# Low parts of the GLU blocks on VectorE, and the first terms of the gate weight sums on SyncE's DMA queue

## What is computed

```
proj = x @ w_in + b_in                  # columns: GLU input (2 x 512) | q | k | v | gate logits (2 x 1024)
u = a * sigmoid(g)                      # a, g: the two halves of the GLU input
u = causal depthwise conv of width 31 over u, + b_dw        # 512 channels
y_conv = silu(layer_norm(u)) @ w_conv_out
y_attn = chunked attention (q, k, v) @ w_attn_out
mixed = (sigmoid(gate_1) * y_conv + sigmoid(gate_2) * y_attn) @ w_o + b_o
x = layer_norm(ALPHA * x + mixed); then a grouped mixture of 16 experts, top 2, and layer_norm again
```

## Time and profile before

| | |
|---|---|
| median of three runs | 1167.88 us (1163.9 to 1169.31) |
| the profiled execution | 1162.02 us, its span 1160.2 us |
| TensorE matmuls | 1082.0 us, 93% |
| VectorE | 827.7 us, 71% |
| ScalarE | 556.4 us, 48% |
| GpSimd | 390.0 us, 34% |
| mean granted clock of TensorE | 0.971 |
| DMA | 222.68 MB, mean 192 GB/s |

### The profile page before, as it was taken

One profiled execution on the slowest core, in us unless ns is written; L12 is line 12 of the kernel. 1 busy time (PEld: TensorE's weight loads), 2 busy tenths in 40 slices (PEclk: granted clock), 3 DMA queues, 4 the chain that ended last, 5 costly groups with the idle time before them and its releaser, 6 DMA issues.

```text
span 1160.2 us, 17229 instructions
## 1 busy us (share of the span) xinstructions
PE 1082.0 (93%) x5487; PEld 897.8 (77%) x5488; DVE 827.7 (71%) x1186; ACT 556.4 (48%) x854; POOL 390.0 (34%) x326
## 2 busy tenths in 40 slices
PE   9924899999999999999999999989999999999985
PEld 7713788888888888978888888878888888888762
DVE  7992589998456775666487478879579565548766
ACT  6401033434447665555433033468478555557755
POOL 3444453535427685565500000015211211212220
PEclk9967899999999999999999999999999999999997
DMA  8897444545320110153344134689999876699956
GB/s 284 230 223 138 74 144 138 164 144 154 119 69 23 42 60 1 38 226 138 133 167 163 73 145 167 230 342 370 315 324 378 324 232 201 237 354 336 346 169 264
DMA packets 64011, 222.68 MB, mean 192 GB/s; under 512 B 9170, under 2 KB 9554, under 8 KB 61891
## 3 DMA queue, kind: packets, MB, share of 16 engines
q1 hardware_dynamic: 51602, 182.49, 42.8%
q0 software_dynamic: 12336, 39.27, 14.5%
HBM read 189.27 MB, written 49.30 MB: 206 GB/s over the span
## 4 chain that ended last, share of the span: by engine, by line
PE 77%; DMA 7%; POOL 5%; DVE 4%; issue 3%; ACT 2%; SPq 1%; ACTq 0%; DVEq 0%; POOLq 0%
PE ps L679 13%; PE ps L681 13%; PE ps L680 13%; PE ps L1802 9%; PE ps L1804 9%; PE ps L1803 9%; DMA gate_weight_sums<-gate_weight_sums 3%; PE ps L801 2%; DMA dn_raw<-in_wexp 2%; PE ps L787 2%; DMA gate_weight_sums<-in_wblk 2%; PE ps L773 2%; PE ps L1883 2%; POOL gate_weight_sums L628 1%; POOL gate_weight_sums L626 1%
## 5 line engine op out<-in xcount | busy, mean ns | idle before, releaser
L1701 DVE TENSOR_TENSOR gu<-gu (+1 forms) x128 | 148.6, 1219 | 33.6 <-issue 21.2
L1239 DVE SCALAR_TENSOR_TENSOR ps<-u,dw_t,ps 128x1024 f32<-128x1024 f32 x116 | 149.2, 1286 | 2.6
L679 PE MATMUL ps<-xh,wh 128*128 128x512 f32 x256 | 104.6, 409 | 46.3 <-POOL wl L598 43.6
L1802 PE MATMUL ps<-gu,xgh 128*128 x336 | 133.9, 399 | 2.5 <-DVE xgl L2200 2.2
L1695 ACT ACTIVATE gu<-gu (+1 forms) x128 | 124.0, 1047 | 20.4 <-DMA gu<-in_wexp 12.3
L1804 PE MATMUL ps<-gu,xgl 128*128 x336 | 131.7, 392 | 0.0
L1803 PE MATMUL ps<-gu,xgh 128*128 x336 | 131.5, 391 | 0.0
L592 POOL TENSOR_SCALAR pr<-pr,rinv 128x640 f32<-128x640 f32 (+4 forms) x64 | 95.2, 1500 | 77.5 <-DVE rinv L1386 77.4
L680 PE MATMUL ps<-xl,wh 128*128 128x512 f32 x256 | 100.9, 394 | 0.0
L681 PE MATMUL ps<-xh,wl 128*128 128x512 f32 x256 | 100.8, 394 | 0.0
L641 POOL TENSOR_TENSOR ul<-uraw,uh 128x512 fp32r<-128x512 f32 x56 | 73.1, 1356 | 80.1 <-ACT uh L1024 80.1
(11 more groups left out here) (307 smaller groups left out, 2635.7 us busy)
## 6 DMA issues: line engine op xcount, KB each, us to landing
gu<-in_wexp SPq DMA_DIRECT2D x64, 1024.0 KB, 9.0
dn_raw<-in_wexp SPq DMA_DIRECT2D x16, 2048.0 KB
raw<-in_wblk SPq DMA_DIRECT2D x36, 512.0 KB, 4.3
gate_weight_sums<-in_wblk POOLq DMA_DIRECT2D x48, 256.0 KB, 5.5
uraw<-gate_weight_sums SPq DMA_DIRECT2D x32, 256.0 KB, 2.9
gate_cols<-gst SPq DMA_DIRECT2D x32, 256.0 KB, 3.2
uraw<-in_wblk SPq DMA_DIRECT2D x24, 256.0 KB, 2.7
xf<-acc_rows SPq DMA_DIRECT2D x8, 512.5 KB, 8.2
```

The costliest lines, as they stand in the source:

```text
L679: pe.matmul(o, a_h, b_h, start=first, stop=False)
L1239: dve.scalar_tensor_tensor(out=so_far if k < CW - 1 else cv[:, j, :], in0=tap, scalar=w, in1=so_far, op0=ALU.mult, op1=ALU.add).then_inc(c ...
L1701: eng.tensor_tensor(gu[:, par, k, 1, :], gu[:, par, k, 1, :].bitcast(F32), gu[:, par, k, 0, :], ALU.subtract).then_inc(gu_lo, 1)
L1802: pe.matmul(o, a_h, b_h, start=first, stop=False)
```

## The change

The first terms are copied by SyncE's queue, group 0 ahead of the load of block 4 and groups 1 to 3 behind the loads of blocks 4 to 6, each after a wait until the group before has landed (`copy_in`). GpSimd keeps the adds, in six rounds, round r waiting for group r of the copies as well, and does them before anything else; the low parts of units 0 to 3 are put between rounds 3 to 5. The low parts of blocks 3 to 7 move to VectorE: block 3 before the input sums, block 4 after their low parts, blocks 5 to 7 in the steps n = 2 to 4 ahead of the taps, of which these steps have seven instead of eight. Units whose sums are now complete a round earlier wait for a round less. The input sums count in `c_sum`, so that its other counts move by four.

```diff
         def sum_round(x, q):
-            return q // 2 + {5: 1, 7: 1, 6: 2, 3: 3}[x]
+            return q // 2 + {5: 0, 7: 0, 6: 1, 3: 2}[x]
         def sums_issued(r):
-            return sum(2 * many for g in range(KC // 2) for stage, many in enumerate((4, 2, 1, 1)) if g + stage <= r)
+            return sum(2 * many for g in range(KC // 2) for stage, many in enumerate((2, 1, 1)) if g + stage <= r)
...
                 sp.dma_start(x1_dram[0:1, :], zeros[0:1, 0:D]).then_inc(zero_out, 16)
+                def first_terms(g):
+                    if g:
+                        sp.wait_ge(copy_in, 16 * 8 * g)
+                    for q in (2 * g, 2 * g + 1):
+                        for i, (n, k) in enumerate(((1, 0), (0, 0), (0, 0), (0, 1))):
+                            sp.dma_start(wsum_dram[i, q], gate_weights(q, n, k)).then_inc(copy_in, 16)
+                first_terms(0)
                 for n in range(RING, B_V[0]):
                     load_block(n)
+                    if n < RING + 3:
+                        first_terms(n - RING + 1)
...
                 def weight_sums(g, stage):
                     if not 0 <= g < KC // 2:
                         return
+                    if stage == 0:
+                        pool.wait_ge(copy_in, 16 * 8 * (g + 1))
                     for q in (2 * g, 2 * g + 1):
                         s1, s2, s3, s4 = (wsum_dram[i, q] for i in range(4))
-                        of = (((s1, gate_weights(q, 1, 0)), (s3, gate_weights(q, 0, 0)), (s2, gate_weights(q, 0, 0)), (s4, gate_weights(q, 0, 1))),
-                              ((s1, gate_weights(q, 1, 1)), (s3, gate_weights(q, 1, 0))), ((s2, s1),), ((s4, s2),))[stage]
-                        for o, a in of:
-                            if stage:
-                                pool.dma_start(o, a, accum_op=ALU.add, max_dma_last_dim=4096).then_inc(wsum_in, 16)
-                            else:
-                                pool.dma_start(o, a).then_inc(wsum_in, 16)
+                        for o, a in (((s1, gate_weights(q, 1, 1)), (s3, gate_weights(q, 1, 0))), ((s2, s1),), ((s4, s2),))[stage]:
+                            pool.dma_start(o, a, accum_op=ALU.add, max_dma_last_dim=4096).then_inc(wsum_in, 16)
...
-                    for stage in range(4):
+                    for stage in range(3):
                         weight_sums(r - stage, stage)
...
-                pool.wait_ge(x_hi, KC)
-                pool.wait_ge(w_lo, 3)
-                for n in range(B_V[0] - 3):
-                    low(n + 3)
-                    for r in (2 * n, 2 * n + 1):
-                        if r < KC // 2 + 3:
-                            sums_round(r)
-                for m in range(N_UNITS):
+                for r in range(KC // 2):
+                    sums_round(r)
+                for r in (KC // 2, KC // 2 + 1):
+                    for m in range(2):
+                        unit_low(2 * (r - KC // 2) + m)
+                    sums_round(r)
+                for m in range(4, N_UNITS):
                     unit_low(m)
+                pool.wait_ge(w_lo, B_V[0])
                 for n in range(B_V[0], B_Q[0] + 2):
                     low(n)
...
-                sums_made = [0]
+                sums_made = [4]
...
+                low(3)
                 input_sums()
                 for i in range(4):
                     dve.wait_ge(x_hi, KC + i + 1)
                     dve.tensor_tensor(t_low[i], t_raw[i], t_high[i], ALU.subtract).then_inc(x_lo, 1)
+                low(4)
                 for n in range(2, B_V[0]):
                     if n % 2 == 0:
                         glu(n // 2 - 1)
-                    some_taps(TAPS_A_STEP)
+                    if n + 3 < B_V[0]:
+                        low(n + 3)
+                    some_taps(TAPS_A_STEP - (n + 3 < B_V[0]))
                 glu(CB - 1)
```

More of the change, by code:

```diff
@@ L278, in encoder_layer @@
         wsum_in = sem("wsum_in"); u_in = [sem(f"u_in{i}") for i in range(UNIT_SLOTS)]; u_hi = sem("u_hi"); u_lo = sem("u_lo")
-        t_sum = sem("t_sum"); c_copy = sem("c_copy"); c_sum = sem("c_sum")
+        copy_in = sem("copy_in"); c_copy = sem("c_copy"); c_sum = sem("c_sum")
         row_moved = [sem(f"row_moved{i}") for i in range(TT)]
@@ L329, in sum_round @@
         def sum_round(x, q):
-            return q // 2 + {5: 1, 7: 1, 6: 2, 3: 3}[x]
+            return q // 2 + {5: 0, 7: 0, 6: 1, 3: 2}[x]
         def sums_issued(r):
-            return sum(2 * many for g in range(KC // 2) for stage, many in enumerate((4, 2, 1, 1)) if g + stage <= r)
+            return sum(2 * many for g in range(KC // 2) for stage, many in enumerate((2, 1, 1)) if g + stage <= r)
         U2, W, U3, C22, C11, C12, C21 = range(1, 8)
         def sum_no(which, q):
-            return 7 * q + which
+            return 4 + 7 * q + which
         def glu_bank(n):
@@ L1034, in _ @@
                         for i in range(4):
-                            act.wait_ge(t_sum, i + 1)
+                            act.wait_ge(c_sum, i + 1)
                             act.activation(t_high[i], t_raw[i], ACT.Copy).then_inc(x_hi, 1)
@@ L1255, in input_sums @@
                 def input_sums():
-                    dve.tensor_tensor(t_raw[0], quarter(xraw, 0, 0), quarter(xraw, 0, 1), ALU.subtract).then_inc(t_sum, 1)
+                    dve.tensor_tensor(t_raw[0], quarter(xraw, 0, 0), quarter(xraw, 0, 1), ALU.subtract).then_inc(c_sum, 1)
                     dve.wait_ge(zero_out, 32)
-                    dve.tensor_tensor(t_raw[1], quarter(xraw, 1, 1), quarter(xraw, 0, 1), ALU.subtract).then_inc(t_sum, 1)
-                    dve.wait_ge(t_sum, 2)
+                    dve.tensor_tensor(t_raw[1], quarter(xraw, 1, 1), quarter(xraw, 0, 1), ALU.subtract).then_inc(c_sum, 1)
+                    dve.wait_ge(c_sum, 2)
                     dve.scalar_tensor_tensor(out=t_raw[2], in0=t_raw[0], scalar=-1.0, in1=quarter(xraw, 1, 1),
-                                             op0=ALU.mult, op1=ALU.subtract).then_inc(t_sum, 1)
-                    dve.wait_ge(t_sum, 3)
+                                             op0=ALU.mult, op1=ALU.subtract).then_inc(c_sum, 1)
+                    dve.wait_ge(c_sum, 3)
                     dve.scalar_tensor_tensor(out=t_raw[3], in0=t_raw[2], scalar=-1.0, in1=quarter(xraw, 1, 0),
-                                             op0=ALU.mult, op1=ALU.subtract).then_inc(t_sum, 1)
+                                             op0=ALU.mult, op1=ALU.subtract).then_inc(c_sum, 1)
                 def gate_sums(m):
```

## The result

The changed kernel took 1148.61 us, the median of four runs (1147.27 to 1150.24), against 1166.84 us for the kernel before on the same chip (four runs, the three from before the change among them). The ratio is 0.9845, with a 95% interval of 0.9816 to 0.9875. The forecast was 1148.8 us. The profiled execution took 1147.27 us, with a span of 1145.5.

The account below looks back on a forecast made before the run. TensorE waiting for GpSimd's low parts, queued behind DMA rounds, was taken as the bound: 46.8 us available, 38.8 at VectorE's pace, less 19.7 of stalls, so 19 won. From 1167.9 that gives 1148.8 us, range 1130 to 1162.

Parts of the forecast that it names:

- What bounds the kernel before, and the 46.8 us: TensorE's GLU blocks: 43.6 us waiting for GpSimd's low parts and 3.2 at lower clock, 46.8 us to be had.
- VectorE becomes the pace: VectorE's GLU steps: fourth GLU product would end at 110.2, so at most 38.8 us come back.
- The landing of groups B, C and D: Copy groups on SyncE's queue beside add rounds 0 to 2: landed at 43.3, 61.5 and 82.7 us.
- group A: First eight copies on SyncE's queue, following the zeros: landed at 28.2 us.
- The stalls: VectorE standing at low parts 5, 6 and 7 for late blocks: 2.6, 7.7 and 9.4 us, together 19.7.
- The Trainium skill's rule: DMAs of all issuing engines share 16 engines; copies on SyncE's queue aren't free: gain 19 us, not 38.8.
- TensorE's clock before unit 2: TensorE ahead of unit 2: lower clock adds 1.9 us by block 7's end, hidden; unit 2 starts at 130.0.
- Three taps into 17.9 us of slack: Taps leaving the GLU blocks go among the units on VectorE: 4.0 us into 17.9 of slack, nothing on the path.
- Rival 1: Block loads on SyncE's queue land before VectorE asks: gain 38.8 less up to 8, 1129 to 1137 us; chance 0.18.
- Rival 2: Copies on SyncE's queue cost 1.15 us, not 0.86: gain 10 (case 2 to 12), 1158 us; chance 0.25.
- Rival 3: Copies on SyncE's queue cost per packet, 1.72 us each: unit 2 starts 8 us later, 1176 us; chance 0.07.

Follow-up runs that it names:

- low-parts-only kernel: Against the kernel before: low parts of blocks 3 to 7 on VectorE, all copies and adds still on GpSimd; 1149.27 us, 0.9881.
- copies-only kernel: Against the kernel before: first terms on SyncE's queue, low parts of blocks 3 to 7 still on GpSimd; 1125.84 us, 0.9685.
- the kernel with the loads first: Against the changed kernel: loads of blocks 5, 6 and 7 put ahead of copy groups 1, 2 and 3 in SyncE's queue; 1129.22 us, 0.9718.
- experiment 1: Against the changed kernel: loads of blocks 5 to 7 put ahead of copy groups 1 to 3 in SyncE's queue; 1129.22 us, 0.9718.
- experiments 2: Each half of the change alone against the kernel before: low parts on VectorE, 0.9881; first terms on SyncE's queue, 0.9685.
- experiment 5: Against the copies-only kernel: block loads put ahead of copy groups 1 to 3; 1128.61 us, 0.9684.
- experiment 4: Against the kernel with the loads first: one tap fewer in each of six steps, 0.9701; then also round 5 behind low parts of units 4 to 9, 0.9695.

## Why the prediction was right

By its own steps:

- **What bounds the kernel before, and the 46.8 us.** Right. With GpSimd's low parts off the path these waits are gone in the change and in the low-parts-only kernel. The waits weren't the whole story of the second half, though: TensorE could have been supplied by GpSimd too (copies only).
- **VectorE becomes the pace, at most 38.8 us.** Right in kind and size for this order of work: with the loads first unit 2 starts at 111.5, 37.6 us before today's 149.0, with 2.0 us of idle left ahead of low part 7. Glu and tap durations were as taken (15 taps in 19.84 us again).
- **The landing of groups B, C and D.** Predicted at 43.3, 61.5 and 82.7 us; the rounds began at 45.4, 63.6 and 84.1. Most of the shift is group A, landed at 29.4 and not at 28.2. The steps were 15.1, 18.2 and 21.2, measured 15.7, 18.2 and 20.6.
- **The stalls.** Predicted 2.6, 7.7 and 9.4 us, measured 4.84, 7.76 and 9.03: 19.7 against 21.6. The first is larger because group B landed late and because VectorE's first GLU product ran at 41.07 and not at 41.9. Their cause, the load's place behind the copies, was shown by experiment 1, and their path, through VectorE's taps, by experiments 2 and 5.
- **The Trainium skill's rule** (DMA: Bandwidth & Descriptors, Issuing engines are not separate DMA queues): copying everything twice shows that a copy on SyncE's queue costs 0.87 us alone and 1.04 in the steps with adds, where it had cost 0.86 on GpSimd's queue. The trace agrees with the rule: nothing of the transfer is saved. The page's 207 to 214 GB/s for HBM-to-HBM copies (Latency and other measured facts) are for rows of 16 KiB at row pitches of 512 KiB and over, which the prediction left out; they would be 1.23 us a copy by estimate. 256 KB in 0.87 us are 301 GB/s, so for these copies the measurement is the one to go by.
- **TensorE's clock before unit 2.** This step failed. The prediction counted the lower clock ahead of block 7 only and took the 4 us wait between units 1 and 2 as free of it. The windows behind 131.05 show 2.5 us lost there. So the 18.0 us of unit 2 became 15.3 at the mark. The medians differ by 18.2 us, close to the forecast of 19, within an interval of 14.6 to 21.5; by the profiles' marks the forecast was some 4 us too good. That the median came within 0.2 us of the one forecast is luck.
- **Three taps into 17.9 us of slack.** The term was mis-sized. Idle time of VectorE over the whole stage isn't slack at its end. In the trace before, the last column sum begins at 284.44 and ends at 285.9, 9.8 us ahead of the mark; after the change it ends 1.7 us ahead of it (275.68 + 2.98 = 278.66 against 280.4). Three taps fewer in the GLU blocks put the last tap two units later, and a unit is 2.7 us of TensorE. It didn't decide here, but the same effect, with six taps more, made experiment 4 come to nothing:

```profile
284.44 1.46 DVE L1247 TENSOR_TENSOR csum<-csum,cv 128x1024 f32<-128x1024 f32 x1
```

```profile
275.68 2.98 DVE L1255 TENSOR_TENSOR csum<-csum,cv 128x1024 f32<-128x1024 f32 x1
```

- **Rival 1** (loads not late) didn't happen; its time, 1129 to 1137, is that of the kernel with the loads first. **Rival 2** had the right sign, at 1.04 against 1.15 us, and only in the steps with adds. **Rival 3** is excluded by group A's 0.87 us. At twice 0.86 us a copy it priced unit 2 at 8 us later than before; the doubled copies showed 13.9 us (162.9 against 149.0) and 1.0162, more than the 1176 / 1167.9 = 1.007 priced.

The rest of the span behind the mark differs by up to 9 us between profiles of kernels that are alike there. For two of them the traces say where. In the copies-only kernel (863.6 us behind the mark) the granted clock was 0.83 and 1.00 in the two stretches of 10 us from 690.1 on; in the same kernel with the loads first (871.3 us) it was 0.62 and 0.53 in the two from 688.3 on, at the same place of the work. By estimate from these four values that is some 7 us of full clock, most of the 7.7 between them, and more than the 1.8 that experiment 5 had won at the mark. Left open is what makes the clock stay low there in one profile and not in the other; no run was made for it.

## What to carry to other kernels

Ask of every moved instruction what stands behind it in its new queue, engine queues and DMA queues alike: a load that lands 10 us late costs next to nothing behind an engine with time to spare, and 9 us behind the one that sets the pace. A prefetch belongs behind the loads that are due sooner, even when it is the older work. Before taps, or any filler, are shifted out of a critical stage, look where the filler as a whole comes due and behind what its last piece then stands, and read the slack there and not as idle time summed over a stage.

## What was not expected

- The two halves of the change, each alone against the kernel before, give 0.9881 and 0.9685, and together 0.9845. One half had the better version of the whole in it.
- After 4.18 us of waiting between two units TensorE ran at 1.2 GHz for 5.3 us. In the copies-only kernel it fell to it for 3.3 us behind a wait of 2.77, where nobody needed the time, and not at all behind the 1.46 us ahead of unit 2. The kernel that reached unit 2 1.9 us later reached the mark 0.9 us earlier.
- In the steps with adds a copy on SyncE's queue cost 1.04 us of time until landing, alone 0.87.
- Six taps moved out of the GLU blocks won nothing while VectorE had 9.6 us idle among the units: its last two taps stood behind TensorE's last unit.
- A wait that the trace put to GpSimd's low parts, and in the kernel with the loads first to "issue", was for VectorE's GLU product. The end times next to the wait tell them apart.
